# The small expert jobs of a mixture-of-experts layer as unsplit fp32 products in two half-width array tiles

## The reference, cut to what matters

```python
def moe_swiglu(h, w_router, w_gu, w_down):
    def fn(t):
        logits = (t @ w_router).astype(jnp.float32)
        top_v, top_i = lax.top_k(logits, TOP_K)
        top_w = jax.nn.softmax(top_v, axis=-1)
        gate = jnp.sum(jax.nn.one_hot(top_i, N_EXPERTS) * top_w[..., None], axis=1)
        gu = jnp.einsum('nd,edf->nef', t, w_gu)
        act = jax.nn.silu(gu[..., :FFN_EXPERT]) * gu[..., FFN_EXPERT:] * gate[..., None]
        return jnp.einsum('nef,efd->nd', act, w_down)
```

## Time and profile before

| | |
|---|---|
| median of 3 runs | 1428.18 us (1427.38 to 1431.02) |
| profiled execution: span on the core | 1429.3 us |
| TensorE busy, its granted clock | 1390.5 us (97%), 0.990 |
| VectorE, ScalarE busy | 1181.7 us (83%), 1021.1 us (71%) |
| HBM read over the span | 429.40 MB, 301 GB/s |

### The profile page before, as it was taken

One profiled execution on the slowest core, in us unless ns is written; L12 is line 12 of the kernel. 1 busy time (PEld: TensorE's weight loads), 2 busy tenths in 40 slices (PEclk: granted clock), 3 DMA queues, 4 the chain that ended last, 5 costly groups with the idle time before them and its releaser, 6 DMA issues.

```text
span 1429.3 us, 19030 instructions
## 1 busy us (share of the span) xinstructions
PE 1390.5 (97%) x6964; PEld 1141.0 (80%) x6964; DVE 1181.7 (83%) x1094; ACT 1021.1 (71%) x1072; POOL 41.2 (3%) x99
## 2 busy tenths in 40 slices
PE   7999999999999989999999999999999999999996
PEld 7987888888974568788888878888878888887884
DVE  6946655547758769899999999999999999999997
ACT  6546544435548857788887878887888888788884
POOL 7000000001000000000000000000000000000000
PEclk9999999999989989999999999999999999999999
DMA  8543555554620038899999999999999999999995
GB/s 324 168 172 118 206 177 189 170 200 148 236 93 27 1 133 316 327 383 420 408 403 402 394 399 404 402 413 397 392 397 398 409 415 396 387 417 385 421 421 216
DMA packets 59995, 431.68 MB, mean 302 GB/s; under 512 B 6656, under 2 KB 6656, under 8 KB 7808
## 3 DMA queue, kind: packets, MB, share of 16 engines
q1 hardware_dynamic: 59760, 429.95, 76.8%
q10 hardware_dynamic: 144, 0.52, 0.1%
HBM read 429.40 MB, written 1.05 MB: 301 GB/s over the span
## 4 chain that ended last, share of the span: by engine, by line
PE 92%; DVE 4%; ACT 1%; issue 1%; DMA 0%; POOL 0%; DVEq 0%; POOLq 0%; SPq 0%; ACTq 0%
PE bank L1516 19%; PE bank L1518 19%; PE bank L1517 19%; PE bank L1995 7%; PE bank L1996 7%; PE bank L2074 3%; PE bank L2014 3%; PE bank L2015 3%; DVE w_lo L1383 2%; PE bank L1864 2%; PE bank L1890 2%; PE bank L1966 1%; PE bank L1874 1%; PE bank L2061 1%; PE bank L1980 1%
## 5 line engine op out<-in xcount | busy, mean ns | idle before, releaser
L1383 DVE TENSOR_TENSOR w_lo<-raw,w_hi 128x2048 fp32r<-128x2048 f32 x331 | 746.2, 2287 | 38.9 <-ACT w_hi L765 36.6
L765 ACT ACTIVATE w_hi<-raw 128x2048 fp32r<-128x2048 f32 x331 | 630.1, 1919 | 128.5 <-PE bank L1518 52.5
L1516 PE MATMUL bank<-w_hi,ht_hi 128*128 128x512 f32 (+1 forms) x768 | 299.3, 390 | 0.9 <-DVE ht_lo L914 0.9
L1518 PE MATMUL bank<-w_hi,ht_lo 128*128 128x512 f32 (+1 forms) x768 | 296.3, 386 | 0.0
L1517 PE MATMUL bank<-w_lo,ht_hi 128*128 128x512 f32 (+1 forms) x768 | 295.8, 385 | 0.0
L882 DVE TENSOR_TENSOR w_lo<-raw,w_hi 128x2048 fp32r<-128x2048 f32 x73 | 166.6, 2289 | 109.7 <-ACT w_hi L446 109.5
L446 ACT ACTIVATE w_hi<-raw 128x2048 fp32r<-128x2048 f32 x74 | 141.6, 1919 | 95.1 <-PE bank L1518 92.8
L1995 PE MATMUL bank<-w_hi,ht_hi 128*128 128x512 f32 x448 | 177.4, 396 | 1.4 <-DVE w_lo L1383 1.4
L1996 PE MATMUL bank<-w_lo,ht_hi 128*128 128x512 f32 x448 | 174.8, 390 | 0.0
L1516 PEld LDWEIGHTS bank<-w_hi,ht_hi 128*128 128x128 f32 x768 | 144.4, 188 | 29.4 <-issue 1.4
L1518 PEld LDWEIGHTS bank<-w_hi,ht_lo 128*128 128x128 f32 x768 | 144.3, 188 | 29.5
(11 more groups left out here) (341 smaller groups left out, 1670.7 us busy)
## 6 DMA issues: line engine op xcount, KB each, us to landing
raw<-in_moe SPq DMA_DIRECT2D x336, 1024.0 KB, 7.5
raw<-in_wts SPq DMA_DIRECT2D x71, 1024.0 KB, 4.9
xs<-in_x SPq DMA_DIRECT2D x2, 512.0 KB, 4.0
out<-xn SPq DMA_DIRECT2D x4, 256.0 KB, 2.0
pk<-in_packed SPq DMA_DIRECT2D x1, 517.0 KB, 8.0
g1b<-in_norm_ffn ACTq DMA_DIRECT2D x1, 512.0 KB, 3.5
gfb<-in_norm_final SPq DMA_DIRECT2D x1, 512.0 KB, 8.4
```

Of the source, the lines that this page charges most:

```text
L765: a(w_hi[:, n % SPLIT, :], raw[:, n % RAW, :], ACT.Copy).then_inc(s_hi, 1)
L1383: v.tensor_tensor(w_lo[:, n % RAW, :], raw[:, n % RAW, :], w_hi[:, n % SPLIT, :].bitcast(F32), ALU.subtract).then_inc(s_lo, 1)
L1516: mm(out_, sh, mh, start=first, stop=False)
L1518: return mm(out_, sl, mh, start=False, stop=last)
```

## The change

Slots of B jobs are no longer split: the matmuls read the landed fp32 slot itself. The 64 places are the stationary operand, in fp32 (`xb`, `at_b`), and each weight block of a k tile is cut into two halves of columns ("sides"), whose outputs go to partitions 0 to 63 and 64 to 127 of the same bank. A B up slot is then 4 k tiles by 2 sides of 256 columns, a B down slot 2 k tiles by 2 sides of 512 columns, each product a two-pass fp32 one. With gate and up of a chunk in 256 columns by 128 partitions, silu and product are done once on 128x256, and two transposes turn a chunk (`turned_b`); ScalarE copies the result to `at_b`. `fold`, its products, `high_b`, `low_b` and `last_down` go. A B job's result is one 128x512 tile `y_b`, gated on the way out of PSUM; its scatter is four fp32 products with 64 rows each in place of eight fp32r ones with 128. ScalarE's and VectorE's `split` pass over B slots (`is_split`), the ring of `w_hi` counts split slots only, and TensorE waits on the landing for B slots (`wait_raw`) and on the split for A slots (`wait_split`). The loads, their order and the rings' sizes stay.

```diff
             def split(m):
-                while nxt[0] <= m and (up is not None or nxt[0] < length):
+                while nxt[0] <= min(m, length - 1 + (TURN if gather is not None else 0)):
                     n = first + nxt[0]
-                    act.wait_ge(landed[n % RAW], i * (16 * 2 * JOB_SLOTS // RAW) + 16 * (n // RAW + 1))
-                    act.wait_ge(s_used, i * (2 * JOB_SLOTS) + (n - SPLIT + 1))
-                    a(w_hi[:, n % SPLIT, :], raw[:, n % RAW, :], ACT.Copy).then_inc(s_hi, 1)
+                    if is_split(n):
+                        act.wait_ge(landed[n % RAW], i * (16 * 2 * JOB_SLOTS // RAW) + 16 * (n // RAW + 1))
+                        act.wait_ge(s_used, hi_freed(i, n))
+                        a(w_hi[:, hi_order(n) % SPLIT, :], raw[:, n % RAW, :], ACT.Copy).then_inc(s_hi, 1)
                     nxt[0] += 1
...
-            def silu_b(c, plus):
-                act.wait_ge(s_bt, (i + plus) * 7 + (c + 1))
-                a(sgt[:, c % 2, :], B[4 + c % 2][:, 0:4 * CAP_B], ACT.Silu).then_inc(s_bsilu, 1)
+            def silu_b(c):
+                if c >= 2:
+                    act.wait_ge(s_bact, i * 7 + (c - 1))
+                a(sgb[:, c % 2, :], B[0][:, 0:256], ACT.Silu).then_inc(s_bsilu, 1)
+
+            def turned_b(c):
+
+                act.wait_ge(s_bt, i * 7 + (c + 1))
+                src = B[4 + c % 2][:, 0:256].rearrange("p (b o t) -> p o b t", b=2, o=2)
+                a(at_b[:, 4 * c:4 * c + 4, :].rearrange("p (o b) t -> p o b t", o=2), src, ACT.Copy).then_inc(s_bat, 1)
...
+                else:
+                    used(length - 1)
+                    a(y_b[:], B[0 if up is None else 2][:, :], ACT.Copy, scale=gcol[:, 1:2]).then_inc(s_yb, 1)
...
+            def product_b(c):
+                dve.wait_ge(s_used, i * (2 * JOB_SLOTS) + (first + up_slot(c, 1, 1, paired) + 1))
+                dve.wait_ge(s_bsilu, i * 7 + (c + 1))
                 if c >= 2:
-                    dve.wait_ge(s_bhi, (i + plus) * 7 + (c - 1))
-                    dve.wait_ge(s_blo, (i + plus) * 7 + (c - 1))
-                v.tensor_tensor(avt[:, c % 2, :], sgt[:, c % 2, :], B[4 + c % 2][:, 4 * CAP_B:8 * CAP_B],
-                                ALU.mult).then_inc(s_bact, 1)
+                    dve.wait_ge(s_bt, i * 7 + (c - 1))
+                v.tensor_tensor(avb[:, c % 2, :], sgb[:, c % 2, :], B[1][:, 0:256], ALU.mult).then_inc(s_bact, 1)
...
         def gu(i, n, s, bank, kind):
...
-                    both = ht_hi[:, 4 + kk // 2, block]
-                    mm(bank[:, :], both, weights(w_hi, n, 512)[:, k, :], start=kk == 0, stop=False)
-                    ins = mm(bank[:, :], both, weights(w_lo, n, 512)[:, k, :], start=False, stop=kk == 7)
+            else:
+
+                wait_raw(i, n)
+                for k in range(4):
+                    kk = 4 * half + k
+                    for side in range(2):
+                        ins = mm(bank[64 * side:64 * side + 64, 0:256], xb[:, kk, :],
+                                 weights(raw, n, 512)[:, k, 256 * side:256 * side + 256], start=kk == 0, stop=kk == 7)
...
+                wait_raw(i, n)
+                pe.wait_ge(s_bat, i * 7 + (d // 2 + 1))
                 for k in range(2):
...
+                    for side in range(2):
+                        ins = mm(B[to][64 * side:64 * side + 64, :], at_b[:, 2 * d + k, :],
+                                 weights(raw, n, 1024)[:, k, 512 * side:512 * side + 512],
+                                 start=d == 0 and k == 0, stop=d == 13 and k == 1)
...
-            def folded(c):
-                pe.wait_ge(s_bg, i * 7 + (c + 1))
-                pe.wait_ge(s_bu, i * 7 + (c + 1))
+            def turned_b(c):
+
+                pe.wait_ge(s_bact, i * 7 + (c + 1))
...
-                for half, src in enumerate((sg, av)):
-                    for j in range(4):
-                        to = (4 * half + j) * CAP_B
-                        ins = mm(B[4 + c % 2][:, to:to + CAP_B], src[:, c % 2, j * P:(j + 1) * P], fold[:],
-                                 start=True, stop=True)
+                for b in range(2):
+                    ins = nc.tensor.transpose(B[4 + c % 2][:, b * P:(b + 1) * P], avb[:, c % 2, b * P:(b + 1) * P], ident[:])
...
+                else:
+                    own = slice(64 * half, 64 * half + 64)
+                    mm(B[b][:, :], selt[own, 1, t * P:(t + 1) * P].bitcast(F32), y_b[own, :], start=True, stop=True).then_inc(s_scat, 1)
```

More of the change, by code:

```diff
@@ L232, in job_slot, with splits_before, is_split, hi_order @@
         return moe[e, s, :, :].rearrange("e p n -> p (e n)")
+    def splits_before(n):
+        r, m = divmod(n - N0 - UP_SLOTS, 2 * JOB_SLOTS)
+        if r < 0:
+            return n
+        d = max(m - JOB_SLOTS, 0)
+        return N0 + UP_SLOTS + r * JOB_SLOTS + min(m, JOB_SLOTS) // 3 + 2 * (d // 3) + d % 3
+    def is_split(n):
+        return splits_before(n + 1) > splits_before(n)
+    def hi_order(n):
+        r = max((n - N0 - UP_SLOTS) // (2 * JOB_SLOTS), 0)
+        return splits_before(n) + r * (-JOB_SLOTS % SPLIT)
+    def hi_free(n):
+        p = n - 1
+        while not is_split(p) or hi_order(p) > hi_order(n) - SPLIT:
+            p -= 1
+        return p + 1
+    def hi_freed(i, n):
+        if isinstance(i, int):
+            return hi_free(n + i * (2 * JOB_SLOTS))
+        return i * (2 * JOB_SLOTS) + (hi_free(n + 4 * JOB_SLOTS) - 4 * JOB_SLOTS)
     def weights(buf, n, b):
-        ring = {id(raw): RAW, id(w_lo): RAW}.get(id(buf), SPLIT)
-        return buf[:, n % ring, :].rearrange("p (a b) -> p a b", b=b)
+        at = hi_order(n) % SPLIT if buf is w_hi else n % RAW
+        return buf[:, at, :].rearrange("p (a b) -> p a b", b=b)
     def head(n):
@@ L786, in phase @@
                 if up is None:
-                    split(min(down_slot(m, paired) + AHEAD, length - 2))
                     if m == 0:
-                        high_b(6, 0)
+                        turned_b(6)
                     continue
@@ L801, in phase @@
                     if c == 0 and down == 1:
-                        high_b(6, 0)
+                        turned_b(6)
                 elif h == 0:
                     split(last + AHEAD)
+                    if c == 0:
+                        high_a(6, 0)
                     used(last)
[L806 to L810, removed]
+                    silu_b(c)
                     if c:
-                        high_b(c - 1, 0)
-                    else:
-                        high_a(6, 0)
+                        turned_b(c - 1)
                 else:
                     split(last + AHEAD)
[L817 to L823, removed]
                 if m == 3 and down is not None:
@@ L1423, in phase @@
                 if up is None:
-                    split(min(down_slot(m, paired) + AHEAD, length - 2))
-                    if m == 0:
-                        low_b(6, 0)
                     continue
@@ L1434, in phase @@
                     split(last + AHEAD)
-                    if c == 0 and down == 1:
-                        low_b(6, 0)
                     product_a(c)
                 elif h == 0:
-                    if c:
-                        split(last + 2)
-                        product_b(c - 1, 0)
                     split(last + AHEAD)
@@ L1445, in phase @@
                 else:
-                    split(last + 1)
-                    if c:
-                        low_b(c - 1, 0)
                     split(last + AHEAD)
+                    product_b(c)
                 if down is None and m < 3:
@@ L2095, in phase @@
                         turned(6, 0)
-                if up is None and m == DOWN_SLOTS - 1:
-                    last_down(i, first + down_slot(m, paired))
-                elif up is None and m >= 2:
+                    if h == 0 and c and up == 1:
+                        turned_b(c - 1)
+                if m == 0 and down == 1:
+                    turned_b(6)
+                if up is None and m >= 2:
                     down_part(i, first + down_slot(m, paired), m, down, 0)
```

232 lines of the change are left out of this document (92 added, 140 removed).

## The result

The kernel after takes 1410.73 us (median of 4 runs, 1409.66 to 1414.46), the one before in the same comparison 1428.79 us (1427.38 to 1431.02). The ratio is 0.9874, with a 95% interval of 0.9857 to 0.989: faster by 18.1 us, where 23.6 were forecast.

What follows compares the result with a forecast made beforehand. TensorE was taken to set the paired phases, with DMA loads and VectorE close behind; 1429.3 less 13.7 (rounds) less 10.4 (last stretch) plus 0.5 (end) gave a 1405.7 us span, median 1404.6, range 1387 to 1440.

Steps and rivals of the forecast that it cites:

- step 6: End of the kernel: without a split the last slot is used about 1.9 us after landing, not 8.4.
- Step 1: B slot matmuls: two array tiles run side by side, 1.80 us an up slot, 1.76 a down slot, before 1.86.
- Step 2: Array width switches between A and B slots: 0.34 us a round trip, 14 in a phase, 4.8 us added.
- Step 3: Folds removed at 1.84 us a chunk: 11.0 us per B-up phase, 1.8 per A-up; transposes return 1.5 and 0.25.
- Step 4: ScalarE and VectorE lose the B slots' splits: nothing gained or lost in paired phases, new waits light.
- Step 5: Scatter as eight 64-row fp32 records in two row tiles: no change in phases, 0.5 us added at the end.
- The sum: Expert part: three rounds save 13.7 us, the last stretch 10.4, the end costs 0.5, giving a 1405.7 us span.
- Rival (d): Loads do not hold 2.50 us a slot but take 2.60, at 403 GB/s: 1419 us; chance 0.17.
- The median: Whole kernel: the profiled span before lies 1.1 us above the runs' median, so the forecast median is 1404.6 us.

Runs made afterwards that it cites:

- the regrouping: Changed kernel with A-up phase slots ordered up, up, down, down, up, up instead of up, up, down: 1405.52 us, ratio 0.9837.
- half-loads kernel: Changed kernel loading only the first half of each B slot, which TensorE reads twice: 1385.66 us, ratio 0.9693.

## Why the prediction was right, and where it was off

The sign and the main causes hold: the slots cost what the array's two tiles allow, A-up phases got longer, B-up phases stopped at the loads, and the last stretch saves most. One cause was sized too large, VectorE's share in the end of before (step 6). Faster had 0.76, and 1410.7 us lies in the range, 6.1 above the forecast. By its steps:

*Step 1, the B slot.* Sized 1.80 and 1.76 us, measured 1.73 for both: an extra of 0.010 a pair doesn't show. Saves TensorE 2 us a B-up phase, of which the loads let nothing through.

*Step 2, the switch.* Sized 0.34. The timeline above has 839.21 to 842.81 for two B up slots, 3.60 us less 2 x 1.73 = 0.14, and the A slot after them ran to the next B product at 845.75, 2.94 less 2.72 = 0.22: 0.36 there and back; the regrouping gives 0.33.

*Step 3, the folds.* The half-loads kernel bears the 6 x 1.84 us out, to within half a microsecond. Its B-up phase is TensorE's own time, and the forecast's 101.2, less 2.0 for the slots, less 1.1 of waiting that the phase of before held, plus 0.3 for the switches at 0.36, is 98.4, as measured; at the 0.33 of the regrouping it is 98.0. The same sum for the A-up phase gives 114.1 or 113.7, and 113.4 was measured, so some term of it is a few tenths too high, and which one is open. Leaving three quarters of the fold products out of before took less than three quarters of it: 5.3 us of busy time for 8.3, and 0.75 us of an A-up phase for 1.4. The busy time is the less sure of the two: a product's record lasts 0.39 us and the next starts 0.23 after it, so up to 0.16 us of every wait counts as busy, and waits are more frequent in that run. By the A-up phase the cost isn't in proportion to the products; what of it a group costs however small it is stays open.

*Step 4, ScalarE and VectorE.* Their lost splits gave nothing in the A-up phases, where TensorE was and is busy all the time; no wait on `turned_b`, `product_b` or `at_b` shows.

*Step 5, the scatter.* The row tiles do overlap:

```profile
1050.30 1.99 PE L2129 MATMUL bank<-y_b,selt 64*128 64x512 f32 x8
1052.22 0.65 PE L2036 MATMUL bank<-ident,av 128*128 128x128 f32 x4
```

1.92 us for eight records, 1.86 before. The 0.5 us at the end isn't there, 10.9 us both times.

*Step 6, the end.* 1.9 us from landing to use, measured 2.0:

```profile
1392.59 1.94 PE L2009 MATMUL bank<-raw,at_b 128*64 128x512 f32 x8 [0.55 <-DMA raw<-in_moe]
...
1395.05 1.94 PE L2009 MATMUL bank<-raw,at_b 128*64 128x512 f32 x8 [0.53 <-DMA raw<-in_moe]
...
1397.04 0.69 ACT L866 ACTIVATE y_b<-bank,gcol 128x512 f32<-128x512 f32 x1 [23.10 <-PE bank L2009]
```

TensorE waits for each landing, 2.46 to 2.49 us apart. The reason given for the 8.4 of before, VectorE behind the loads, was right for 1.5 of the 6.5 us between the two kernels; the rest is the split chain itself, its two copies ahead of the products, and the longer products. The sum didn't need the reason, since it put the 1.9 us in from the unsplit products alone.

*The sum* failed in two terms. First, "a round takes 215.45 for 220.0, and three save 13.7" took one B-up phase for all. The first of before was 103.6 us and not 107.6: no finished job is there to scatter in it, which saves 1.9 us, and it has none of the 1.1 us of waiting; the last 1.0 is open. Its pair takes 216.0, and 4.0 us of the 13.7 never stood to be saved. A table of the stretches of all phases, not of one of each kind, would have shown it. Second, "the A-up phase lets them run ahead, 4.2 landed slots, and the B-up phase eats that up": the stock was 3 or 4 slots at the end of an A-up phase and 2 or 3 at the end of a B-up one. The 4.3 us split chain keeps the last ones. Of 42 landings in a B-up phase, at 2.52 us a slot 105.8 us, the phase undercuts only 2.8, so it takes 103 and not 101.2; the rounds measured 215.5, 216.3 and 217.0, together 2.5 us over the forecast. Two errors cancel in part in these 2.5: the three B-up phases came out 5.0 us over it, the three A-up phases 2.5 under. 4.0 and 2.5, and 0.1 since the third pair of before took 219.9, are the 6.6 us between the 13.7 forecast and the 7.1 saved. The last stretch has the same error: 53 landings at 2.48 us and 2.0 give 133.4, measured 133.1; 51.8 at 2.50 were taken, 131.4.

*Rival (d)*, loads that don't hold 2.50 us: they hold 2.48 us a slot in the last stretch and 2.51 to 2.56 in the B-up phases, 417 to 419 GB/s. In A-up phases they move 395 to 399, but there TensorE takes 2.70 us a slot and they follow it.

*The median.* The profiled execution of before was taken as 1.1 us above the median; the lost clock makes it slower than most, and the span leaves out time (1.8 us between span and device time in that of after). With these 1.8 us it would be the run at 1431.02 us, 2.8 above the median, and 2.8 less 1.8 is the 1.1 that was taken, up to rounding. That the forecast kept the lost clock in both kernels does no harm to the difference. In sum, the rounds saved 6.6 us less than forecast, the last stretch 1.7 less and the tail 0.5 more: 7.8 between 23.6 and 15.8. The medians differ by 2.3 more than the expert part, and that part of the agreement is luck, no merit of the working.

## What to carry to other kernels

An engine that is busy all the time may have the next bound within 5% of it: a change that saves its work is worth only what that next bound leaves, and to price it one asks how much stock the ring can truly give up, which is the slots less those under way and less those that stand in a chain behind their landing. Work out a sum over phases from every phase, not from one that stands for all; the first and last differ. And where slots of two widths alternate, group them, but look first at what scatter and gather stand beside: the same 7 switches fewer a phase cost 9 us in one order, some 3 of them by the clock, and gave 5 in the other.

## What the runs showed of the hardware that was not expected

- Two 64-column fp32 tiles that stream different data overlap entirely: 0.216 us for a pair of 256 columns, with one tile 1674.95 us for the whole against 1410.73.
- A 1 MB load landed 4.8 us after its issue in the one-tile kernel, 7.5 in before, 8.5 after, and 9.9 in B-up phases after, while the slots came every 3.4, 2.6, 2.6 and 2.5 us. Divided, that is an estimate of 1.4, 2.9, 3.3 and 3.9 loads under way: the time to landing grows with them. How few would hold 2.5 us a slot no run shows.
- The granted clock of TensorE fell to its lower level for 10 us (a mean of 0.54 over the stretch) in one execution and not in another of the same attention part, though both hold the same wait of 2.1 us there, at a cost of 4.7 us: over a fifth of the 21.4 us between the two profiled spans.
- In the expert part it fell for 3.4 or 6.8 us at or just behind waits of 2.0 to 3.1 us of TensorE, twice in one order of the slots and four times in another, and never in the kernel after. So an order that makes TensorE wait can cost more than the wait.
